# All four score blocks of a head in one step, a third PSUM bank for them, and two receiving buffers for the turned probabilities

## The reference

```python
SEQ, CHUNK, ATT_HEADS, ATT_HEAD_DIM = 512, 64, 8, 64
scores = jnp.einsum("bnqhd,bnkhd->bnhqk", qc, kb) * (dh ** -0.5)
bias = rel_bias[:, jnp.clip(dist, -REL_CLIP, REL_CLIP) + REL_CLIP]
scores = jnp.where(valid, scores + bias[None, None], NEG_INF)   # keys of 9 chunks: causal by chunks
p = jax.nn.softmax(scores, axis=-1)
out = jnp.einsum("bnhqk,bnkhd->bnqhd", p, vb)
...
y = jnp.concatenate([ya * jax.nn.silu(ag), yr * jax.nn.silu(rg)], axis=-1)   # yr: 4 retention heads
return x + y @ w_out
```

## Time and profile before

| | |
|---|---|
| timed runs | 1249.45, 1250.77, 1253.47 us, median 1250.77 |
| the profiled execution | 1247.33 us, of which the span from first to last instruction is 1245.5 us |
| granted TensorE clock, mean | 0.984 |
| busy in the span | PE 1207.9, PE weight load 1022.6, DVE 861.3, ACT 585.3, POOL 294.0 us |
| DMA | 135.33 MB, 109 GB/s over the span |

### The profile page before, as it was taken

One profiled execution on the slowest core, in us unless ns is written; L12 is line 12 of the kernel. 1 busy time (PEld: TensorE's weight loads), 2 busy tenths in 40 slices (PEclk: granted clock), 3 DMA queues, 4 the chain that ended last, 5 costly groups with the idle time before them and its releaser, 6 DMA issues.

```text
span 1245.5 us, 15736 instructions
## 1 busy us (share of the span) xinstructions
PE 1207.9 (97%) x5901; PEld 1022.6 (82%) x5901; DVE 861.3 (69%) x1425; ACT 585.3 (47%) x1048; POOL 294.0 (24%) x299
## 2 busy tenths in 40 slices
PE   8999999999999999999999998889999998889998
PEld 7888888888888888888888886788888896779886
DVE  5789655556875677457757986857748786867656
ACT  5666332333442344144444676534535666545442
POOL 0220599902000000000026921212305111211310
PEclk8999999999999999999999998999999999989999
DMA  6422333333323333333323465553215464552221
GB/s 180 136 68 68 94 102 94 92 102 100 122 79 106 111 92 102 102 89 97 102 85 119 127 178 147 146 130 85 69 38 165 126 178 137 156 131 69 69 84 68
DMA packets 207697, 135.33 MB, mean 109 GB/s; under 512 B 5418, under 2 KB 200452, under 8 KB 207492
## 3 DMA queue, kind: packets, MB, share of 16 engines
q1 hardware_dynamic: 207620, 134.32, 37.4%
HBM read 121.72 MB, written 12.58 MB: 108 GB/s over the span
## 4 chain that ended last, share of the span: by engine, by line
PE 75%; DVE 9%; DMA 8%; issue 3%; ACT 2%; SPq 2%; DVEq 0%; ACTq 0%
PE ps L191 74%; DMA b_px<-turned 7%; SPq L197 2%; DVE wlo L164 2%; DVE b_pd L182 2%; PE ps L194 1%; ACT b_pt L161 1%; DVE b_p L178 1%; DVE b_sets L164 1%; DVE b_pt L164 1%; DVE tmp L164 1%; DMA xtm<-in_x_dram 1%; DVE x1l L164 0%; DMA raw<-in_w_in_dram 0%; ACT whi L161 0%
## 5 line engine op out<-in xcount | busy, mean ns | idle before, releaser
L161 ACT ACTIVATE whi<-raw 128x1024 fp32r<-128x1024 f32 (+1 forms) x198 | 206.4, 1050 | 288.8 <-PE ps L191 277.8
L164 DVE TENSOR_TENSOR wlo<-raw,whi 128x1024 fp32r<-128x1024 f32 (+1 forms) x192 | 245.2, 1283 | 48.9 <-ACT whi L161 48.4
L191 PE MATMUL ps<-x0h,wlo 128*128 128x512 f32 x1008 | 258.8, 396 | 0.0
L191 PE MATMUL ps<-x0h,whi 128*128 128x512 f32 x1008 | 256.3, 393 | 0.0
L191 PE MATMUL ps<-x0l,whi 128*128 128x512 f32 x1008 | 255.3, 391 | 0.0
L191 PEld LDWEIGHTS ps<-x0h,wlo 128*128 128x128 f32 x1008 | 190.5, 191 | 39.0
L191 PEld LDWEIGHTS ps<-x0h,whi 128*128 128x128 f32 x1008 | 188.9, 189 | 38.5
L191 PEld LDWEIGHTS ps<-x0l,whi 128*128 128x128 f32 x1008 | 188.2, 188 | 38.8
L164 POOL TENSOR_TENSOR sums<-sums,sq 128x512 f32<-128x512 f32 x28 | 43.6, 1571 | 423.2 <-ACT sq L161 423.2
L191 PE MATMUL ps<-x1h,wlo 128*128 128x512 f32 x304 | 82.3, 389 | 0.0
L191 PE MATMUL ps<-x1h,whi 128*128 128x512 f32 x304 | 82.3, 389 | 0.0
(11 more groups left out here) (191 smaller groups left out, 1738.4 us busy)
## 6 DMA issues: line engine op xcount, KB each, us to landing
raw<-in_w_in_dram SPq DMA_DIRECT2D x98, 512.0 KB, 4.2
raw<-in_w_up_dram SPq DMA_DIRECT2D x44, 512.0 KB, 3.8
raw<-in_w_out_dram SPq DMA_DIRECT2D x24, 512.0 KB, 4.1
turned<-b_pd SPq DMA_DIRECT2D x16, 640.0 KB, 2.9
b_px<-turned SPq DMA_DIRECT2D x64, 160.0 KB, 5.1
raw<-in_w_down_dram SPq DMA_DIRECT2D x16, 512.0 KB, 4.2
raw<-in_w_down_dram SPq DMA_DIRECT2D x8, 384.0 KB, 3.4
xtm<-in_x_dram SPq DMA_DIRECT2D x4, 512.0 KB, 7.2
```

The costliest lines, as they stand in the source:

```text
L161: return AC.put(lambda e: e.activation(o, i, func, **kw), after, AC, 1)
L164: return on.put(lambda e: e.tensor_tensor(o, a, b, op), after, on, 1)
L191: return PE.put(lambda e: e.matmul(o, l, r, start=start, stop=stop), after, PE if mark else None, 1)
```

## The change

The pool of probability buffers becomes three buffers with three users that share their release tokens: heads write their probabilities always to buffer 0 (`hps`), the read-back goes to buffer 2 (the old `b_px`) and buffer 1 in turn (`pxs`), and retention heads take 0 and 1 in turn (`rps`). The read-back has two semaphores instead of one. Tile 1's scores go to bank 6, in the same step as the others; `biased` of all four tiles is in one step and `soft` of all four in the next. A `ret` is entered on the agenda a step earlier with an empty first step, which leaves it in its old step but behind work that was put there earlier. The new offsets of a head are: 0 all scores, 1 all `biased`, 2 all `soft`, 3 reciprocal and scalings, 4 block transposes and the DMA out, 6 the four DMAs in, 11 high part, 12 low part, 13 the matmuls with the values. The next bias load moves from offset 3 to 1.

```diff
 class Slots:
-    def __init__(self, aps):
-        self.aps, self.free, self.i = aps, [[] for _ in aps], -1
+    def __init__(self, aps, ids=None, free=None):
+        self.aps, self.i = aps, -1
+        self.ids = range(len(aps)) if ids is None else ids
+        self.free = [[] for _ in aps] if free is None else free
     def take(self):
         self.i += 1
-        k = self.i % len(self.aps)
+        k = self.ids[self.i % len(self.ids)]
...
-        d_px = Counter(sem("s_px"))
+        d_px = [Counter(sem(f"s_px{i}")) for i in range(2)]
...
-        pbs = Slots([PB[:, 0:1280], PB[:, 1280:2560]])
+        p_bufs, p_free = [PB[:, 0:1280], PB[:, 1280:2560], PX[:, :]], [[], [], []]
+        hps, pxs, rps = Slots(p_bufs, [0], p_free), Slots(p_bufs, [2, 1], p_free), Slots(p_bufs, [0, 1], p_free)
...
-                outs = {3: PS[3][:, :], 0: PS[4][:, 0:128], 2: PS[4][:, 128:512], 1: PS[3][:, 0:256]}
-                tp3 = score(3, outs[3], claim(3))
+                outs = {3: PS[3][:, :], 0: PS[4][:, 0:128], 2: PS[4][:, 128:512], 1: PS[6][:, 0:256]}
+                tps = {3: score(3, outs[3], claim(3))}
                 free = claim(4)
                 score(0, outs[0], free)
-                tp2 = score(2, outs[2], free)
+                tps[0] = tps[2] = score(2, outs[2], free)
+                tps[1] = score(1, outs[1], claim(6))
+                if e == 1:
+                    qk_free[s % 2] = q_read[s] = [tps[1]]
                 yield 1
...
-                kp, pb, pfree = pbs.take()
+                kp, pb, pfree = hps.take()
...
-                tm = {3: biased(3, tp3)}
-                bank_free[3] = [tm[3]]
-                tm[0], tm[2] = biased(0, tp2), biased(2, tp2)
-                bank_free[4] = [tm[2]]
-                yield 1
-                tp1 = score(1, outs[1], claim(3))
-                if e == 1:
-                    qk_free[s % 2] = q_read[s] = [tp1]
-                for t in (3, 0, 2):
-                    te = soft(t, tm[t])
-                yield 1
-                tm[1] = biased(1, tp1)
-                bank_free[3] = [tm[1]]
+                tm = {t: biased(t, tps[t]) for t in (3, 0, 2, 1)}
+                bank_free[3], bank_free[4], bank_free[6] = [tm[3]], [tm[2]], [tm[1]]
...
                 if i < 6:
                     load_bias(i + 2)
                 yield 1
-                te = soft(1, tm[1])
+                for t in (3, 0, 2, 1):
+                    te = soft(t, tm[t])
                 yield 1
...
-                pbs.free[kp] = [tb]
+                hps.free[kp] = [tb]
...
                 yield 2
+                kx, px, xfree = pxs.take()
                 back = spot.rearrange("(j p) (d x) -> d p j x", j=4, d=4)
                 for d in range(4):
-                    t_px = dma(PX[32 * d:32 * d + 32, :].rearrange("p (j x) -> p j x", j=4), back[d], d_px,
-                               after=[t_out, px_free[0]])
+                    t_px = dma(px[32 * d:32 * d + 32, :].rearrange("p (j x) -> p j x", j=4), back[d], d_px[kx // 2],
+                               after=[t_out, xfree])
                 spot_free[i % 2] = [t_px]
-                yield 3
+                yield 5
                 _, pt, tfree = ptbs.take()
                 hi, lo = pt[:, 0:1280], pt[:, 1280:2560]
-                th = act(hi, PX[:, :], after=[t_px, tfree])
+                th = act(hi, px, after=[t_px, tfree])
                 yield 1
-                tl = tt(lo, PX[:, :], f32(hi), ALU.subtract, after=[t_px, th, tfree])
-                px_free[0] = [th, tl]
-                yield 2
+                tl = tt(lo, px, f32(hi), ALU.subtract, after=[t_px, th, tfree])
+                pxs.free[kx] = [th, tl]
+                yield 1
...
+            def a_step_later(work):
+                yield 1
+                yield from work
...
-                at_step(n, ret(i))
+                at_step(n - 1, a_step_later(ret(i)))
```

More of the change, by code:

```diff
@@ L1091, in block_then_hybrid_layers @@
         AT_K = [0, 4, 7, 9]
-        pd_free, px_free, spot_free = [[]], [[]], [[], []]
+        pd_free, spot_free = [[]], [[], []]
         SPOT = [nc.dram_tensor(f"turned_{i}", (128, 1280), F32).ap() for i in range(2)]
@@ L1372, in ret @@
                 yield 1
-                kp, pb, pfree = pbs.take()
+                kp, pb, pfree = rps.take()
                 t0 = decay(0, o0, tp0)
@@ L1426, in ret @@
                     tp = tr(PS[7][:, 128 * t:128 * t + 128], ob[t // 2][:, t % 2, :], IDENT, after=[t5[t], free], mark=t == 3)
-                pbs.free[kp] = [tp]
+                rps.free[kp] = [tp]
                 yield 1
@@ L1455, in layer_b @@
             for i in range(1, 8):
-                at_step(12 + 6 * i, head(i))
+                at_step(13 - l + 6 * i if i == 0 else 12 + 6 * i, head(i))
             evs = []
```

## The result

The changed kernel takes 1208.34 us (median of 4 runs, 1206.91 to 1208.67) against 1250.11 for the kernel before (4 runs, 1248.63 to 1253.47): a ratio of 0.966, 95% interval 0.9639 to 0.9681. The forecast was 1220 with a range from 1209 to 1238. The direction and the mechanism were right; the size was too small (30.9 us forecast, 41.8 measured), and the range missed the time by 0.7 us. The profiled execution took 1208.31, its span is 1206.5 us, its mean clock 0.994.

What follows compares the result with a forecast made beforehand. PE sets the pace, interrupted in the attention heads by 27.2 us of waits traced to the late read-back. Idle 25.1 less 4.0 new waits plus 9.8 clock gives 30.9 us: 1250.8 to 1220, range 1209 to 1238.

Steps and rivals of the forecast that it cites:

- The chain of causes: Attention heads: late read-back makes ACT, DVE, `biased` and bank 3 late in turn; PE waits 27.2 us together.
- Rival 3: Read-back still late, ACT waiting 2 to 3 us a head: 1236 us, chance 0.09.
- lag of SP: Head at 1034.75: SP issues the read-back 4.8 us after the DMA out, behind two raw loads waiting for `wlo`.
- moving the read-back doesn't shorten its landing: Read-back on its queue: by the ring-order rule it is served after raw loads ahead; landing 5.1 us median, 7.86 behind two.
- Scores and bank 6: removed 13.5 us: Tile 1's score at offset 2: its own bank ends PE's waits for bank 3, 13.5 us.
- I put 4 us on this: Value matmuls at offset 13 instead of 14: 4 us of new waits over 16 heads, between 0 and 30.
- Rival 1: Attention heads: DVE becomes the limit and values wait; about 14 us gained, 1237 us, chance 0.11.
- Exps and scalings in consecutive steps: Offsets 2 and 3 of a head: DVE waits for ACT 0 to 3 us a head, costed at nothing further.
- Rival 2: Exp and scalings in consecutive steps stop DVE twice a head: slower, about 1275 us, chance 0.04.
- Clock: Slowed matmul groups behind PE's waits in the heads: 9.8 of 12.65 us come back.
- the median of the timed runs lies 3.5 above it: Conversion from profiled execution (1247.3 before, 1216.4 forecast) to the median of timed runs: 3.5 us added.
- all idle and clock back (39.8 us) gives 1211: Best case of the forecast's own range: 39.8 us gained, 1211 us.

Runs made afterwards that it cites:

- asking later: Kernel before, old banks, DMAs in at 8; high part at 13, low part 14, values 16 except in heads 7; two receiving buffers: 1213.8 us, ratio 0.9685.
- the delayed kernel: Changed kernel with the four DMAs in (the read-back) at offset 8 instead of 6, all else the same: 1231.5 us, ratio 0.9844.

## Why the forecast had the direction and missed the size

**The chain of causes was right.** Read-back late, ACT late, DVE late, bank 3 late: asking later removes all of it in heads 0 to 6 with the old banks, and delaying the read-back in the changed kernel brings 23 us back. Rival 3 (the read-back stays late) is what the delayed kernel does. The "lag of SP" was read from one of four heads with two loads (4.8 us); the median is 3.6 us, of which SP's own lag behind the landed DMA out is 0.6. And the inference that moving the read-back doesn't shorten its landing failed: it went from 5.1 to 3.6 us, in a kernel where the moved DMAs no longer follow a raw load directly.

**"Scores and bank 6: removed 13.5 us" named the wrong owner.** The bank alone gives none of it. As long as the read-back is late, what is given at the bank is taken back at the values; asking later removes the same 13.5 us (0.3 are left) without the bank. In the whole change the sum is the same, so this didn't cost the forecast, but it would have for the bank alone.

**"I put 4 us on this", the values one step earlier: measured nothing.** PE waits 0.3 us in all for the low part of `b_pt` in the changed kernel, and a step later is 4 to 6 us slower. I took DVE's lag from traces in which DVE was held by ACT and kept part of it; without that hold it had none of consequence. Rival 1 (DVE the limit) falls with it: DVE is busy 93.57 of 105 us in layer 1, 89% (I had 86% for both layers), and PE has no wait. The one wait that came, 3.6 us at head 2, is another: transposes moved ahead of operands, on a DVE slowed beside POOL. My list had only 1.2 us there.

**Exps and scalings in consecutive steps** cost nothing that PE sees, as forecast: DVE's reciprocals waited 2.2 us in all for ACT's `b_p`, in three heads. Rival 2 didn't occur. Its price had an error of its own: 55 us lost less 27 gained make 1279 from 1250.8, not 1275.

**The sum, term by term.** Idle: forecast 27.2 to 6.1, measured 27.2 to 3.9, 2.2 more. Clock: forecast 9.8. In the changed kernel the slow groups from 719.50 on still hold 2.8 of the 12.65, so 9.85: right. Not in the sum at all: a group of matmuls overlaps the next by 0.17 us (1.20 long, 1.03 to the next start in the earlier trace rows), and each wait loses that too; PE has 17 waits fewer (5 against 22), which I estimate at 2.9 us. The first 40 us were 1.4 shorter in this execution, before any changed instruction. That is luck: after nearly the same wait for an input, matmuls ran at the slow clock in the kernel before and at full clock in the changed one, here the same two matmuls before and after:

```profile
12.68 1.20 PE L191 MATMUL ps<-x0h,whi 128*128 128x512 f32 x2
```

```profile
12.44 0.70 PE L191 MATMUL ps<-x0h,whi 128*128 128x512 f32 x2
```

That makes 37.4 of the 39.0 us between the two profiled executions; 1.6 stay unassigned. The last 2.8 of the 41.8 between the medians is the step "the median of the timed runs lies 3.5 above it": the profiled execution of before was a quick one of its kind (1247.3; the other runs of that kernel reach from 1247.6 to 1255.3 over all groups), that of the changed kernel is at its median. I treated the distance as fixed.

**The step that failed: "all idle and clock back (39.8 us) gives 1211".** This was the bound on which the lower end of the range, 1209, stood, and it was no bound: the medians are 41.8 us apart with 3.9 us of waits and 2.8 us of slow clock still there. It was made of idle time and clock alone. The sum put the overlap that each wait loses (2.9 us) at nothing, and took the distance from the profiled execution to the median as fixed, which was off by 2.8. With the 2.2 us of idle that the term of 4 us cost, the 1.4 us of luck and the 1.6 us unassigned, these are the 10.9 us between the gain of 30.9 and that of 41.8. So the mechanism held and its size was wrong; that the time lies just outside the range and not just inside is within the luck of the runs.

## What to carry to other kernels

When an engine that works in order waits for a transfer, look first at how many steps lie between issue and use, and at what stands ahead of the issue on its queue; the waits of the other engines, a shared bank among them, may be only where the lateness arrives. A fix at that place alone can be worth less than nothing (0.4% slower here), and be worth something once the root is gone (9 us). When you forecast new waits from lags of the old trace, ask first whether the lag is itself the thing that goes; and when you bound a gain by the idle time, add what each wait costs beside its idle time.

## What the runs showed that I had not expected

A DVE subtraction of 64x512 from SBUF took 1.3 us in the mean while POOL ran its scalings of 128x512 and 0.7 us when they were moved away (5.29 against 2.83 us for four, the two rows above). Not every one beside POOL is slow: in the changed kernel the ten that ran almost wholly beside POOL work took 0.67 to 1.78 us each, the 37 alone 0.67 to 0.69.

The landing of the read-back went with how far ahead the last weight load was issued: 5.3 us under 0.6 us, 3.6 us at 2 to 3. And a wait of 1.74 us left no slow matmuls behind in one kernel, while one of 1.76 us, just ahead of 755.67 in the earlier trace rows, did in the kernel before: waits near that size may or may not cost clock.
